# Mixer's output projection taken into the merge's block, and a reordered way from its output to the experts' block table

## The chip, the cores and the metric

The kernel runs on one core of one Trainium2 chip. Its time is the device time of one execution in microseconds (us); a kernel's figure is the median of its runs. The clock of TensorE has two levels, 1.2 and 2.4 GHz; the profile gives the granted clock of a stretch as a share of the upper one.

## What is computed

A block with a token mixer and 64 routed experts, followed by a second block. Only the end of the mixer and the start of the expert stage matter here (512 tokens, width 1024, all float32):

```python
mix, mix_c = token_mixer(...)            # ends in merged @ w_out
x = x + gt1 * rmsnorm(mix, g_post_mix[li])
h = modulate(rmsnorm(x, g_pre_ffn[li]), sh2, sc2)
...
top_g = lax.top_k(grp_score, TOPK_GROUPS)[1]          # 4 of 8 groups
top_e = lax.top_k(jnp.where(emask, sel, -jnp.inf), TOP_K)[1]   # 8 of 64 experts
wts = jnp.take_along_axis(scores, top_e, axis=1)
wts = wts / jnp.sum(wts, axis=-1, keepdims=True) * ROUTED_SCALE
# each expert's tokens are padded to blocks of 128; a table says which token sits in which row
dest = pstart[e_sorted] + jnp.arange(n_assign, dtype=jnp.int32) - start[e_sorted]
buf_tok = jnp.zeros((n_pad,), jnp.int32).at[dest].set(tok_sorted)
...
shared = (jax.nn.silu(h @ w_sh_gate) * (h @ w_sh_up)) @ w_sh_down
```

## The kernel before

The program is written engine by engine, in blocks. Between two blocks all engines meet at a barrier; inside a block they are ordered by semaphores alone. `clear_sems` (L102) clears the semaphores that were used so far, and adds a barrier of its own. Products of full precision are made of three matmuls of rounded parts (`mm3`, L283): every operand is kept as a high part, which ScalarE copies into the rounded type, and a low part, the difference, which VectorE takes. For weights this is the work of `SplitRing`: four raw slots that SyncE fills by DMA, and two pairs of buffers for the parts, so that the parts of tile n need tile n-2 to be used up (`high` L229 to L237, `low` L241 to L248).

The stages around the change, in order of time:

- `merge` (L2790): for each of 8 column tiles (i) four products of 24 matmuls, two for gates and two for the attention and SSD branches; ScalarE takes the sigmoids (L2884), VectorE writes `mergedT[:, i]` (L2953 to L2955). Beside it POOL and VectorE make the late modulation rows in `c.x`, and then POOL loads x again (L2836).
- `project_residual` (L434): merged times w_out, 8 contraction tiles, 4 token tiles and 2 halves of 512 columns, 192 matmuls. The left side is split in two halves (L495, L521) into the buffers of the attention's output. The order is: both column halves for the first four contraction tiles, then for the last four, one half after the other. Only then are the 8 banks copied (L526), squared (L507), the norm's factors made for all tokens at once (L528, L529, POOL L513), and x updated (L533, L538).
- `clear_sems`, then `norm_transpose` (L296): squares of x (L324), factors (L342, POOL L337), scaling (L348), 8 transposes for a token tile (L370), and the way out of the banks with gain and shift by VectorE (L355) and ScalarE (L330) into `hT`. Beside it SyncE runs `ahead` (L3066): the router's weights, constants, the shared expert's weights, and the first expert's weights.
- `experts` (L2981). TensorE: router logits (L3287), 32 matmuls with `hT` as the stationary side and 64 columns; transposes back to token order for the gather (L3294), each tile after ScalarE's copies (L3449) of the one before; then the ranks and counts of the chosen experts (L3305, L3307), the block counts (L3313 to L3315) and the shared expert (L3299, L3332). VectorE: scores, top 4 groups and top 8 experts (L3528 to L3562), the weights `wt` (L3565 to L3569), the keys (L3571, L3573), the counts (L3576 to L3581), the places `dest` (L3584 to L3596), and for each token tile `pick_tile` (L3600 to L3605). POOL: 8 indirect DMAs for a token tile scatter rows into the block table in HBM (L3210), 32 in all, after which the table is loaded (L3212) and the first tokens are gathered (L3192). The expert loop of TensorE begins with the transposes of these rows (L3274).

The second block has the same kind of projection, with a form of the tail that is already written tile by tile: `Rows` (L778), `Turn` (L798), `Residual` (L836), `Tail` (L875), used by `project_norm` (L966). In `Tail` a token tile is squared, normed, added and turned while the next one is multiplied.

```python
    def pe(self, pe, product):
        c, turn = self.c, self.turn
        product(0)
        product(1)
        product(2)
        turn.turn(c, pe, 0)
        product(3)
        turn.turn(c, pe, 1, True)
        turn.turn(c, pe, 2)
        turn.turn(c, pe, 3)
```

## Time and profile before

| | |
|---|---|
| runs | 3293.53, 3294.71, 3296.37 us; median 3294.71 us |
| profiled execution | 3292.3 us |
| span from first to last instruction of that execution | 3290.6 us |
| mean granted TensorE clock | 0.951 |
| PE busy | 3006.1 us (91%) |
| VectorE, ScalarE, POOL busy | 1809.3, 1418.8, 536.1 us |
| chain that ended last | TensorE 11%, all the rest rounds to 0% |

In the profile PE is TensorE's matmuls, PEld its weight loads, DVE is VectorE, ACT ScalarE, POOL GpSimd, SP SyncE; PEq or POOLq is an engine's sequencer. A line such as L3210 is a line of the kernel. One fp32 matmul leaves two matmul records, one of rounded parts leaves one. Times of rows are from the span's start.

### The profile page before, as it was taken

How to read it: one execution, taken by the hardware profiler on the slowest of the kernel's cores; microseconds unless marked ns; L12 is line 12 of the kernel's file. 1: busy time of each engine (PE TensorE's matmuls, PEld its weight loads, DVE VectorE, ACT ScalarE, POOL GpSimd, SP SyncE). 2: the span in 40 equal slices, each digit the busy share in tenths (PEclk: the TensorE clock that was granted, in tenths of full speed). 3: DMA queues.
4: the chain of work that ended last, by engine and by line, in shares of the span. 5: the costliest groups of instructions: out<-in, count | busy, mean ns of one | idle time of the engine just before them, and what ended most of it. 6: DMA issues, size and time to landing. Idle time of an engine off the chain costs nothing. (4 is left out here: it accounts for less than half of the span.)

```text
span 3290.6 us, 37471 instructions
## 1 busy us (share of the span) xinstructions
PE 3006.1 (91%) x14702; PEld 2413.3 (73%) x14702; DVE 1809.3 (55%) x2174; ACT 1418.8 (43%) x1894; POOL 536.1 (16%) x692
## 2 busy tenths in 40 slices
PE   7978899998987799999999689889999899889998
PEld 4866788787876377777777367668887788678887
DVE  4447736445543488888886444555543325445443
ACT  3324526245122288888786122333332334433332
POOL 0005414133100422323222100000000003100000
PEclk9989999998997799999999899889999899999999
DMA  5210201023642279999997630223332211223321
GB/s 193 58 53 1 74 11 52 26 52 122 202 138 90 107 297 367 361 368 373 374 375 299 270 105 1 66 77 103 102 103 77 80 39 52 58 78 90 103 90 51
DMA packets 277406, 455.60 MB, mean 138 GB/s; under 512 B 24656, under 2 KB 206800, under 8 KB 258160
## 3 DMA queue, kind: packets, MB, share of 16 engines
q1 hardware_dynamic: 250832, 398.43, 34.8%
q0 software_dynamic: 26400, 54.79, 4.6%
q8 instruction: 117, 1.92, 0.2%
q14 instruction: 57, 0.47, 0.0%
HBM read 450.77 MB, written 39.08 MB: 149 GB/s over the span
## 5 line engine op out<-in xcount | busy, mean ns | idle before, releaser
L248 DVE TENSOR_TENSOR weight_part<-weights,weight_part 128x2048 fp32r<-128x2048 f32 (+1 forms) x65 | 148.2, 2280 | 166.0 <-ACT weight_part L237 166.0
L288 PE MATMUL banks<-hT_r,weight_part 128*128 128x512 f32 x496 | 200.2, 404 | 4.6 <-PEq L974 2.9
L1133 ACT ACTIVATE up_room<-banks,tap_columns 128x512 f32<-128x512 f32 x88 | 68.6, 779 | 313.9 <-PE banks L293 313.9
L237 ACT ACTIVATE weight_part<-weights 128x2048 fp32r<-128x2048 f32 (+1 forms) x65 | 121.7, 1872 | 174.9 <-PE banks L288 169.4
L1174 DVE SCALAR_TENSOR_TENSOR up_room<-banks,tap_columns,up_room 128x511 f32<-128x511 f32 x88 | 66.0, 750 | 238.5 <-ACT up_room L1133 238.5
L293 PE MATMUL banks<-hT_r,weight_part 128*128 128x512 f32 x496 | 195.5, 394 | 0.0
L248 DVE TENSOR_TENSOR weight_part_o<-weights,weight_part_o 128x2048 fp32r<-128x2048 f32 (+2 forms) x49 | 106.9, 2182 | 143.1 <-ACT weight_part_o L237 143.1
L862 POOL TENSOR_SCALAR branch_mean<-branch_mean 128x1 f32<-128x1 f32 x16 | 3.5, 222 | 1096.7 <-ACT up_room L856 747.2
L288 PE MATMUL banks<-hT_r,weight_part_o 128*128 128x512 f32 x432 | 174.5, 404 | 6.7 <-PEq L105 3.8
L293 PE MATMUL banks<-hT_r,weight_part_o 128*128 128x512 f32 x432 | 170.8, 395 | 0.0
L292 PE MATMUL banks<-h_low,weight_part_o 128*128 128x512 f32 x432 | 169.7, 393 | 0.0
L292 PE MATMUL banks<-h_low,weight_part 128*128 128x512 f32 x432 | 169.0, 391 | 0.0
L3192 POOL DMA_INDIRECT gathered<-h_tokens,block_rows x64 | 115.5, 1805 | 225.0 <-PE banks L3274 206.8
L3269 PE MATMUL banks<-weights_r,gatheredT_r 128*128 128x512 f32 x336 | 133.5, 397 | 0.0
L237 ACT ACTIVATE weight_part_o<-weights 128x2048 fp32r<-128x2048 f32 (+2 forms) x49 | 89.4, 1825 | 98.0 <-PE banks L288 93.7
L288 PEld LDWEIGHTS banks<-hT_r,weight_part 128*128 128x128 f32 x496 | 94.2, 190 | 26.7 <-issue 7.2
L2770 DVE TENSOR_REDUCE minus_maxima<-banks 128x2 f32<-128x1536 f32 x32 | 56.3, 1758 | 97.7 <-PE banks L2679 97.7
L293 PEld LDWEIGHTS banks<-hT_r,weight_part 128*128 128x128 f32 x496 | 93.6, 189 | 22.2
L3517 DVE TENSOR_TENSOR weights_r<-weights,h_tokens_r 128x2048 fp32r<-128x2048 f32 x42 | 95.7, 2291 | 17.5 <-ACT h_tokens_r L3423 17.5
L3268 PE MATMUL banks<-gate_up_high,gatheredT_r 128*128 128x512 f32 x256 | 103.8, 406 | 0.0
L3197 POOL DMA_INDIRECT expert_rows<-lent,block_rows x64 | 65.4, 1022 | 235.3 <-ACT lent L3480 231.3
L3268 PE MATMUL banks<-h_tokens_r,gatheredT_r 128*128 128x512 f32 x256 | 103.2, 403 | 0.0
(725 smaller groups left out, 8977.0 us busy)
## 6 DMA issues: line engine op xcount, KB each, us to landing
weights<-in_w_e_gate SPq DMA_DIRECT2D x44, 1024.0 KB, 15.9
weights<-in_w_e_up SPq DMA_DIRECT2D x44, 1024.0 KB, 18.5
hT<-in_w_e_down SPq DMA_DIRECT2D x44, 1024.0 KB, 18.9
weights<-in_w_up SPq DMA_DIRECT2D x88, 512.0 KB, 5.1
gate_up<-in_w_e_gate SPq DMA_DIRECT2D x22, 1024.0 KB, 15.5
gate_up<-in_w_e_up SPq DMA_DIRECT2D x22, 1024.0 KB, 18.3
down<-in_w_e_down SPq DMA_DIRECT2D x22, 1024.0 KB, 18.4
weights<-in_w_down SPq DMA_DIRECT2D x20, 1024.0 KB, 5.0
```

Source lines behind the costliest of these rows:

```text
L237: c.nc.scalar.activation(self.parts[n % 2][0][:, 0:z], self.raw[n % RAW_SLOTS][:, 0:z], ACT.Copy).then_inc(self.high_ready, 1)
L248: c.nc.vector.tensor_tensor(low[:, 0:z], self.raw[n % RAW_SLOTS][:, 0:z], high[:, 0:z].bitcast(F32), ALU.subtract).then_inc(self.low_ready, 1)
L288: ins = c.nc.tensor.matmul(out, lhs[0], rhs[0], start=start, stop=False)
L292: c.nc.tensor.matmul(out, lhs[0], rhs[1], start=False, stop=False)
L293: return c.nc.tensor.matmul(out, lhs[1], rhs[0], start=False, stop=stop)
L1133: nc.scalar.activation(a[:, f % 2, v], c.ps[:, 2 * (f % 4) + v], ACT.Identity, scale=conv[:, 2, ch:ch + 1], bias=bias[:, ch:ch + 1]).then_ ...
L1174: nc.vector.scalar_tensor_tensor(a[:, f % 2, v, 1:], c.ps[:, 2 * (f % 4) + v, 0:SEQ - 1], conv[:, 1, ch:ch + 1], a[:, f % 2, v, 1:], ALU.m ...
L3192: nc.gpsimd.indirect_dma_start(xg[n % 2][:], None, h_dram, bass.IndirectOffsetOnAxis(tab[:, n, 0:1], 0), bounds_check=SEQ - 1, oob_is_err= ...
L3197: nc.gpsimd.indirect_dma_start(y_dram, bass.IndirectOffsetOnAxis(tab[:, n, 2:3], 0), y[n % 2][:], None, bounds_check=SEQ * TOP_K - 1, oob_ ...
L3268: nc.tensor.matmul(out, lhs[0], rhs[0], start=start, stop=False)
L3269: nc.tensor.matmul(out, lhs[0], rhs[1], start=False, stop=False)
L3517: nc.vector.tensor_tensor(gu_low[i][:, v], gu[i][:, v], gu_high[n % 2][:, v].bitcast(F32), ALU.subtract).then_inc(gu_parted, 1)
```

## The change

Four things are changed; the rest of the program is the same.

1. The projection, the residual and the norm move into the merge's block. `project_residual` and `norm_transpose` go. The weights of w_out follow the merge's own in `SplitRing`; the left side is split in three pieces, contraction tiles 0 to 3, 4 to 6, and 7. The first group is multiplied for both column halves, then the last four contraction tiles are multiplied token tile by token tile in a `Tail` whose outputs are plain (`TurnPlain`, `PlainTail`).
2. `clear_sems` stands ahead of the merge, and no longer behind the projection. The router's and the shared expert's weights are loaded by SyncE at the end of the merge's block (`EarlyExperts`); `ahead` with the rest runs at the start of the experts' block.
3. The router's product has the router's 64 columns as its stationary side and 512 tokens as columns: 8 matmuls, a copy, and four small transposes to token order. The transposes of `hT` use three pairs of banks.
4. On the way to the table, counts come before ranks, ranks are 4 matmuls, the `wt` steps stand behind `dest`, the steps for `over` behind the first `pick_tile`, and the shared expert's matmuls behind the block counts.

```diff
+class TurnPlain(Turn):
+    def weigh(self, c, dve, t):
+        if t >= 2:
+            dve.wait_ge(self.turned, 2 * (t - 1))
+        dve.wait_ge(self.rooted, t + 1)
+        c.nc.vector.tensor_scalar(self.xg[:, t % 2], c.x[:, t], self.rs[:, t:t + 1], None, ALU.mult).then_inc(self.weighted, 1)
...
+class PlainTail(Tail):
...
+    def dve(self, dve):
+        c, res, turn = self.c, self.res, self.turn
+        res.add(c, dve, 0)
+        res.add(c, dve, 1)
+        turn.weigh(c, dve, 0)
+        res.add(c, dve, 2)
+        turn.weigh(c, dve, 1)
+        turn.out_v(c, dve, 0)
+        res.add(c, dve, 3)
+        turn.weigh(c, dve, 2)
+        turn.out_v(c, dve, 1)
+        turn.weigh(c, dve, 3)
+        turn.out_v(c, dve, 2)
+        turn.out_v(c, dve, 3)
...
+        c.clear_sems()
+        merge(c, w_in, h, yT, o_parts, cond, early)
...
                 c.split.load(sp, merge_tiles(c))
-                c.split.ahead(sp, residual_tiles(t["w_out"][0], KD))
+                c.split.load(sp, group_tiles(t["w_out"][0], groups))
+                sp.wait_ge(c.split.low_ready, len(c.split.sizes))
+                early.load(c, sp)
...
+                for hf in range(2):
+                    high, low = group_weights(c, pe, 4)
+                    if hf == 0:
+                        pe.wait_ge(m_low, 1)
+                        pe.wait_ge(left, KD - 1)
+                    for tile in range(NT):
+                        if hf == 0 and tile == 2:
+                            pe.wait_ge(left, KD)
+                        tok = slice(tile * P, (tile + 1) * P)
+                        for j in range(4):
+                            mm3(c, c.ps[:, 2 * tile + hf], [a[:, j, tok] for a in o_parts], (high[:, j], low[:, j]), j == 0, False)
+                pe.wait_ge(m_low, len(pieces))
+                tail.pe(pe, final_product(c, pe, res, [a[:, 4:8] for a in o_parts], 4))
...
+                c.split.high(c, act)
+                act.wait_ge(attn_done, 1)
+                act.wait_ge(left, KD - 1)
+                for n, at in enumerate(pieces):
+                    if n == 2:
+                        act.wait_ge(left, KD)
+                    nc.scalar.activation(o_parts[0][:, at], mT[:, at], ACT.Copy).then_inc(m_high, 1)
+                for _ in range(3):
+                    c.split.high(c, act)
+                tail.act(act)
...
-            pe.wait_ge(landed, 144)
+            pe.wait_ge(early.router_in, 16)
+            for k in range(KD):
+                last = mm1(c.ps[0:E, 0], early.router[:, k], c.hT[:, k], start=k == 0, stop=k == KD - 1)
+            last.then_inc(logits, 1)
+            pe.wait_ge(kept, 1)
             for tile in range(NT):
+                last = nc.tensor.transpose(c.ps[:, 1, tile * E:(tile + 1) * E], by_expert[:, tile * P:(tile + 1) * P], c.ident[0:E, 0:E])
+            last.then_inc(logits_turned, 1)
...
             pe.wait_ge(chosen, 1)
+            pe.wait_ge(landed, 128)
...
-            pe.wait_ge(sh_up_in, 32)
-            shared_up(0, 0, range(0, 2))
             pe.wait_ge(blocked, 1)
...
+            pe.wait_ge(early.up_in, 32)
+            pe.wait_ge(copied, 2 * NT)
+            shared_up(0, 0, range(0, 2))
             shared_up(0, 0, range(2, KD))
```

VectorE at the end of the merge, before (`oT_r` and `oT_low_r` are the parts of the left side, `weight_part` and `hc` the two pairs of weight parts):

```order
L2955 TENSOR_TENSOR mergedT<-mergedT,gated_ssd 128x512
L2798 UNCONDITIONAL_BRANCH
L515 UNCONDITIONAL_BRANCH
L521 TENSOR_TENSOR oT_low_r_3366<-mergedT,oT_r_3365 128x2048
L248 TENSOR_TENSOR weight_part_231<-weights,weight_part_230 128x2048
L248 TENSOR_TENSOR hc_low_r_51<-weights,hc_high 128x2048
```

and now:

```order
L253 TENSOR_TENSOR hc_low_r_51<-weights,hc_high 128x2048
L2828 TENSOR_TENSOR oT_low_r_3366<-mergedT,oT_r_3365 128x2048
L2894 TENSOR_TENSOR gated_ssd<-banks,sigmoids 128x512
L2895 TENSOR_TENSOR mergedT<-banks,sigmoids 128x512
L2896 TENSOR_TENSOR mergedT<-mergedT,gated_ssd 128x512
L2828 TENSOR_TENSOR oT_low_r_3366<-mergedT,oT_r_3365 128x1536
L2828 TENSOR_TENSOR oT_low_r_3366<-mergedT,oT_r_3365 128x512
```

The first weight tile's low part and the first half of the left side stand ahead of the last merge step, and the block's end (the two branches) is gone from between.

TensorE at the start of the experts' block, before (`lent` is a buffer that holds the routing's small arrays):

```order
L3287 MATMUL banks<-weights,hT 128x64 x32
L3294 MATMUL banks<-ident,hT 128x128 x32
L3305 MATMUL banks<-lent 128x64 x10
L3307 MATMUL banks<-lent 64x1 x4
L3299 MATMUL banks<-hT,weights 128x512 x2
L3313 MATMUL banks<-lent 128x64
```

and now:

```order
L3226 MATMUL banks<-hT,weights 64x512 x8
L3230 MATMUL banks<-ident,lent 128x64 x4
L3237 MATMUL banks<-ident,hT 128x128 x32
L3248 MATMUL banks<-lent 64x1 x4
L3250 MATMUL banks<-lent 128x256
L3252 MATMUL banks<-lent 128x192
L3252 MATMUL banks<-lent 128x128
L3252 MATMUL banks<-lent 128x64
L3255 MATMUL banks<-lent 128x64
```

The 32 narrow router matmuls became 8 wide ones, the counts stand ahead of the ranks, and no matmul of the shared expert stands ahead of the block counts.

## Rows read from the trace of the kernel before

**Rows 1.** TensorE in order of time: start, duration, what, [idle before, releaser].

```profile
977.77 0.79 PE L288 MATMUL banks<-weight_part,oT_r 128*128 128x512 f32 x1 [8.84 <-DVE weight_part L248]
...
1045.69 6.43 PE L370 MATMUL banks<-ident,x_scaled 128*128 128x128 f32 x32 [21.06 <-DVE x_scaled L348]
1054.49 13.88 PE L3287 MATMUL banks<-weights,hT 128*128 128x64 f32 x64 [2.37 <-PEq L300]
```

**Rows 2.** ScalarE and VectorE from the scores to the first `pick_tile`.

```profile
1068.41 0.39 ACT L3445 ACTIVATE lent<-banks 128x256 f32<-128x256 f32 x1 [14.23 <-PE banks L3287]
...
1078.02 0.29 DVE L3562 TENSOR_SCALAR lent<-lent 128x256 f32<-128x256 f32 x1
...
1080.14 0.84 DVE L3571 TENSOR_TENSOR_SCAN lent<-lent 128x64 f32<-128x64 f32 x4
...
1087.18 0.15 DVE L3576 COPY lent<-banks 64x1 f32<-64x1 f32 x1 [5.74 <-PE banks L3307]
...
1092.23 0.15 DVE L3592 COPY lent<-banks 64x1 f32<-64x1 f32 x1 [1.23 <-PE banks L3315]
...
1093.76 0.69 DVE L3600 TENSOR_TENSOR lent<-lent 128x512 f32<-128x512 f32 x1
```

**Rows 3.** POOL's scatters into the table, and TensorE's first step of the expert loop.

```profile
1098.22 1.37 POOL L3210 DMA_INDIRECT block_table<-lent  x1 [41.93 <-DVE lent L3605]
...
1121.65 2.93 POOL L3210 DMA_INDIRECT block_table<-lent  x1 [0.31 <-issue]
...
1151.37 1.94 PE L3274 MATMUL banks<-ident,gathered 128*128 128x128 f32 x8 [15.70 <-DMA gathered<-h_tokens,block_rows]
```

**Rows 4.** The page's group of ScalarE's copies of a weight tile: busy, mean ns.

```profile
L237 ACT ACTIVATE weight_part<-weights 128x2048 fp32r<-128x2048 f32 (+1 forms) x65 | 121.7, 1872 | 174.9 <-PE banks L288 169.4
```

**Rows 5.** Stretch: its length, busy (x records) of each engine, PEclk, DMA share, GB/s.

```profile
978.00:983.00 5.00, 5.00 (x13) 3.89 (x14) 2.40 (x2) 3.71 (x2) 0.00 (x0) 0.52 0.00 0
983.00:1025.00 42.00, 41.63 (x181) 33.55 (x179) 11.76 (x11) 8.91 (x16) 0.00 (x0) 1.00 0.00 0
...
1054.40:1068.80 14.40, 14.31 (x67) 14.34 (x68) 0.00 (x0) 0.39 (x1) 1.84 (x2) 0.50 0.67 271
```

**Rows 6.** The second block's `project_norm`, last group and tail, in order of time.

```profile
2138.03 0.40 PE L288 MATMUL banks<-weight_part_o,oT_high 128*128 128x512 f32 x1
...
2142.82 0.50 PE L288 MATMUL banks<-weight_part,oT_high 128*128 128x512 f32 x1 [1.83 <-DVE weight_part L248]
...
2165.28 0.40 PE L293 MATMUL banks<-weight_part,oT_low 128*128 128x512 f32 x1
...
2172.68 1.27 DVE L811 SCALAR_TENSOR_TENSOR tail_rows<-x_tok,rstd,norm_rows 128x1024 f32<-128x1024 f32 x1
...
2174.01 1.97 PE L816 MATMUL banks<-ident,tail_rows 128*128 128x128 f32 x8 [0.42 <-DVE tail_rows L811]
2178.87 0.77 PE L288 MATMUL banks<-hT_r,weight_part_o 128*128 128x512 f32 x1 [2.89 <-PEq L974]
```

**Rows 7.** VectorE and ScalarE in order of time, from the residual to `hT`.

```profile
1032.59 4.63 DVE L538 TENSOR_TENSOR x_tok<-x_tok,yT 128x1024 f32<-128x1024 f32 x4
...
1038.87 1.06 ACT L324 ACTIVATE squares<-x_tok 128x1024 f32<-128x1024 f32 x1 [12.75 <-PEq L105]
...
1050.07 0.74 DVE L348 TENSOR_SCALAR x_scaled<-x_tok,rstd 128x1024 f32<-128x1024 f32 x1
...
1051.28 2.91 ACT L330 ACTIVATE hT<-banks,shift,scale 128x128 f32<-128x128 f32 x8 [0.36 <-PE banks L370]
```

**Rows 8.** The shared expert's fp32 matmuls of 512 columns, two records each.

```profile
1087.00 3.78 PE L3299 MATMUL banks<-hT,weights 128*128 128x512 f32 x4
...
1099.33 20.87 PE L3299 MATMUL banks<-hT,weights 128*128 128x512 f32 x48
```

**Rows 9.** DMA issues from 940 to 1160 us: size, median us to landing.

```profile
lent<-const_table SPq DMA_DIRECT2D x1, 208.0 KB, 6.0
block_table<-lent SPq DMA_DIRECT2D x1, 208.0 KB, 14.8
```

343 lines of the change are left out of this document (120 added, 223 removed).

## The prediction

> **What bounds the kernel now.** I read the page first. TensorE is busy for 91% of the span, so only stretches in which it stands still or is slow can give much. In the slices its granted clock and its busy share fall together at about 1000 to 1150 us, which is the projection's end and the way to the experts. I then read that stretch engine by engine. TensorE's timeline shows the path [rows 1]: it stops at 968.93 with the merge (977.77 less the idle 8.84), starts the projection at 977.77, ends it at 1024.63 (the 1045.69 row less its idle 21.06), waits 21.06 us for the norm, transposes, and starts the router's product at 1054.49. All of this is one chain: each wait is for the last instruction ahead of it. The next group carries it on through VectorE [rows 2]: scores ready at 1068.80, experts chosen at 1078.31, a wait of 5.74 us for TensorE's counts, one of 1.23 us for the block counts, first `pick_tile` at 1093.76. POOL starts its 32 scatters at 1098.22 [rows 3], and the expert loop begins at 1151.37, when the first gathered rows are there. TensorE waited 15.70 us for them, so in that last stretch POOL sets the time and the shared expert lies beside it, with 15.70 us to spare. What is won before 1098.22 moves the whole rest forward; what is won on TensorE behind it is worth nothing.
>
> **The projection and the norm.** Call the start of the router's product T; it is 1054.49 now.
> - From merge to projection. The block's end stands between them now. In the new order the first weight tile's parts and the first half of the left side are made while TensorE still multiplies for the last merge step: attention's product, whose buffers the parts overwrite, ends 5.6 us before the merge's end (24 matmuls at 0.23 us), and ScalarE's copy (1.9 us for such a piece [rows 4]) and VectorE's difference, little longer, fit in that. Token tiles 0 and 1 need banks that are free already, 2 and 3 need the last merge step, which is over 2 us later, while tiles 0 and 1 take 5.5 us. So the 8.84 us go to nothing [rows 1]. With them goes the half clock at the start of the projection: 0.52 in the first 5 us, 1.00 later [rows 5]. At full clock a matmul takes 0.23 us (181 records in 41.63 us); 192 would take 44.4, and took 46.86 (977.77 to 1024.63), so 2.5 us.
> - The first group is 96 matmuls at 0.23 us, 22.2 us, so the last group starts at 968.93 + 22.2 = 991.1.
> - The last group and the tail. The second block runs the same class with the same sizes: from its last group's start, 2138.03, to the next stage, 2178.87, are 40.84 us [rows 6]. In them are a wait of 1.83 us for the second half's weight parts, which the new code has too (the pair of buffers comes free only when the last group begins), and the slow clock behind it. Three things are shorter here. The last tile's scaling takes 0.74 [rows 7] and not 1.27 us [rows 6]; the same on tile 0 brings the first transposes forward, 0.3 us (estimate from that 0.53). Behind the last transposes the second block needs 2.89 us [rows 6]; here ScalarE's four outputs take 1.46 us (half of the eight of 2.91) and the barrier 0.30 (1051.28 + 2.91 to 1054.49) [rows 1, 7], so 1.1 less. That leaves 40.84 - 0.53 - 0.3 - 1.1 = 38.9 us.
> - T = 991.1 + 38.9 = 1030.0, a gain of **24.5 us**. About 11 us of it are the start, the rest is the norm that no longer stands behind the whole product.
>
> **The moved clear.** Where blocks change with a clear, VectorE ends at 1037.22 and ScalarE starts at 1038.87, 1.65 us [rows 7]; without one the barrier is 0.30. The old place is in the 24.5 already. The new one stands ahead of the merge, where TensorE has nothing else: **1.35 us lost**.
>
> **The router.** Now 13.88 us at a granted clock of 0.50, though TensorE is busy all the time [rows 1, 5]. The new form is 8 matmuls of 512 columns. Their price is the shared expert's [rows 8]: 1.89 us at half clock (4 records, two matmuls, in 3.78), 0.87 at full (48 records in 20.87). Before them come transposes at half clock, so I take two at 1.89 and six at 0.87, 9.0 us; the bounds are 7.0 (all full) and 15.1 (all half). Then a copy of 512 columns (0.6, from 0.39 for 256 [rows 2]), four transposes (1.0, half of eight at 1.97 [rows 6]), the sigmoid and the hand-overs (0.6): scores at T + 11.2. Now they are at T + 14.31. Gain **3.1 us**, between 5.1 and -3.0. The Trainium skill (TensorE: Matmul & The Clock Gate, What's actually happening) says that the clock is throttled by default and that activity releases it; the 13.88 us of unbroken matmuls at 0.50 disagree. By that rule the new form takes the 9.0 us and the gain is 3.1; if it goes as the old form did, it is 3.0 lost, and that is the first rival.
>
> **From scores to the first scatter.** The top-k steps are the same: 9.5 us. TensorE's transposes for the gather no longer wait for each copy, and are through about when the experts are chosen. Then the counts are four matmuls of one column, about 1 us (estimate), less than VectorE's scans and keys (1080.14 to 1081.44, where the wait begins: 1.3 us [rows 2]), so the wait of 5.74 goes. Two steps of 0.18 us with their hand-overs (0.15 the bare step [rows 2]) fall away, two of 0.2 go behind the first `pick_tile`. The ranks are 640 columns at 3.7 ns (3.78 us for 1024 [rows 8]), 2.4 us behind the counts; VectorE gets there 1.3 us earlier and waits, in place of the 1.23 for the block counts, which are now made meanwhile. The `wt` steps (1078.31 to 1080.14, 1.8 us [rows 2]) only change places. Gain 5.74 + 0.36 + 0.4 + 1.23 - 1.3 = **6.4 us**.
>
> **At nothing.** The shared expert starts later, behind the block counts: 32 matmuls (two slow) and 16 more, some 50.5 us from the choice, and POOL's rows come at 66.7 (13.5 to the first scatter, which is 1098.22 - 1078.31 less the 6.4, then 53.15 as now), so 16 us of cover stay. Without it each of them would cost its 0.87. The constants are issued at T, 8 DMAs in 4 us, and the last lands 6.0 us behind its issue [rows 9]: T + 10, one us ahead of the scores. The table's first fill (14.8 us [rows 9]) is there by T + 25, the first scatter comes at T + 34. The router's and shared weights are loaded from 996 on, some 30 us before use. The number and length of scatters stay.
>
> **Sum.** 24.5 + 3.1 + 6.4 - 1.35 = 32.6 us, against the profiled execution's 3292.3 us: 3259.7. That execution lies 2.4 us under the median of 3294.71, so for the median I say **3262.1 us**, 1.0% less.
>
> **Rivals.**
> 1. The router stays at half clock. For it: the form now does. Against: the 512-column matmuls of [rows 8] came to 0.87 after a few us. Then 15.1 and not 9.0: 3268.2. Chance 0.10.
> 2. A wait takes the place of the removed ones: the constants. Their DMAs share the rings with 3 MB of weights issued behind them, as the table's first fill does, which took 14.8 us. If the last constant takes that long, it lands at T + 19 and VectorE's first step waits 7.6 us: 3269.7. Against: this constant landed in 6.0 us beside as much traffic [rows 9]. Chance 0.05.
> 3. POOL's small factor steps in the tail wait for VectorE's wide ones. On the last tile's path are two of them; each could wait for at most one instruction of 1.27 [rows 6]: 2.5 us, 3264.6. Against: from the last product's end (2165.68) to the last scaling (2172.68) the second block needs 7.0 us [rows 6], of which nothing looks like a wait. Chance 0.05. The Trainium skill (SBUF — State Buffer, SBUF: two separate sides) states such a rule: VectorE and GpSimd share one pair of ports, and who comes second is blocked for the whole instruction; the 7.0 us agree with it only if no pair meets there.
> 4. Slower: TensorE's clock. If it is granted half from the merge's end on, the 180 matmuls that I count at full clock cost 0.20 us more each, 36 us, the router 6.1 more, and of the shared expert's 45 us more 16 are covered: 3262.1 + 36 + 6.1 + 29 = 3333. It decides from 39.2 us on, that is with projection and router both slow. For it: this stretch has the lowest clock of the program now. Against: there the clock fell in waits, and the projection now follows the merge, at full clock, without one. Chance 0.02.
> 5. The change doesn't do what it says: the tail's order puts a wait on TensorE that leaves the norm behind the product, or the projection is held by the last merge step. Then of the 24.5 only the 11 of the start stay: 3275.6. Against: the second block's rows. Chance 0.03.
>
> **How the numbers follow.** The forecast has 0.75. Its own bounds are the router (2.0 less to 6.1 more), the clock behind the 1.83 us wait (up to 1.6 less if it stays up), the ranks (1 either way), and the scatters, of which one took 2.93 us beside weights being loaded [rows 3], against 1.37 and less: 2 us either way. Range 3254 to 3272, which takes in rivals 1 to 3. A measurement of this kernel tells a change from none at about 0.2%, 6.6 us. Faster by more: 0.96; within: 0.01; slower: 0.03.
>
> **What would show it.** TensorE goes on within 0.3 us of the merge's last matmul and its clock stays at 1.00 until the last group; one wait of about 1.8 us there; 39 us from the last group's first matmul to the router's; the router in 9 us with a clock that rises in it; a wait for TensorE's ranks of about 1.3 us on VectorE and none over 2 us; 32 scatters and 54 us from the first fill to the expert loop, unchanged; 1.7 us between the stages ahead of the merge. I am wrong if TensorE waits again between merge and projection, if more than 7 us lie from the last product to the last scaling, or if the distance from POOL's first scatter to the expert loop grows.

## The result, and the profile of the changed kernel

The changed kernel takes 3259.73 us (median of 4 runs, 3258.22 to 3264.65) against 3294.55 us for the kernel before in the same comparison: ratio 0.9897, 95% interval [0.9882, 0.9911]. It is faster by 1.0%. The forecast was 3262.1 us, with 3254 to 3272 as its range. The profiled execution took 3258.77 us, with a span of 3257.1 us (before: 3292.3 and 3290.6) and a mean granted clock of 0.958 (0.951).

The path around the merge's end first, TensorE in order of time with the two rows of ScalarE and VectorE that stand between (start, duration, what, [idle before, releaser]), in the changed kernel:

```profile
786.08 0.76 PE L293 MATMUL banks<-hT_r,hc_high 128*128 128x512 f32 x1 [2.82 <-PEq L110]
...
996.71 0.50 PE L293 MATMUL banks<-weight_part,oT_r 128*128 128x512 f32 x1 [1.82 <-DVE weight_part L253]
...
1018.98 1.03 ACT L669 ACTIVATE y_high<-banks 128x1024 f32<-128x1024 f32 x1 [2.94 <-PE banks L298]
...
1025.89 0.75 DVE L760 TENSOR_SCALAR y_high<-x_tok,rstd 128x1024 f32<-128x1024 f32 x1 [0.31 <-POOL rstd L608]
...
1030.17 7.05 PE L3226 MATMUL banks<-hT,weights 128*64 128x512 f32 x16 [1.84 <-PEq L2693]
```

The 8.84 us between merge and projection and the 21.06 us behind it [rows 1] are gone: from the first matmul of the merge to the last of the projection TensorE waits once for over 1 us, 1.82 us for the second half's weight parts; behind that product the tail's waits for scaled tiles come to some 5 us. Stretch by stretch (length, busy time and records of PE, PEld, DVE, ACT and POOL, PEclk, DMA share, GB/s):

```profile
970.00:991.00 21.00, 21.00 (x92) 17.08 (x91) 8.81 (x7) 4.36 (x3) 0.00 (x0) 1.00 0.00 1
998.00:1019.50 21.50, 21.50 (x97) 17.40 (x96) 10.13 (x12) 7.34 (x15) 3.96 (x10) 0.94 0.47 157
1019.50:1030.10 10.60, 3.88 (x19) 3.01 (x17) 7.78 (x16) 7.20 (x18) 2.38 (x6) 0.84 0.00 0
1030.10:1037.30 7.20, 7.05 (x16) 2.11 (x16) 0.00 (x0) 0.04 (x1) 1.84 (x2) 1.00 0.19 52
```

The start of the projection runs at 1.00, where it was at 0.52 [rows 5], and so does the router's product, which was at 0.50. Then the way to the first scatter and to the expert loop, in order of time:

```profile
1038.40 0.38 ACT L3391 ACTIVATE lent<-banks 128x256 f32<-128x256 f32 x1 [0.55 <-PE banks L3230]
...
1040.19 0.42 DVE L3474 TENSOR_TENSOR lent<-lent 128x256 f32<-128x256 f32 x1 [10.97 <-DMA lent<-const_table]
...
1053.23 0.42 DVE L3525 TENSOR_SCALAR lent<-banks 128x256 f32<-128x256 f32 x1 [1.32 <-PE banks L3252]
...
1063.28 1.12 POOL L3150 DMA_INDIRECT block_table<-lent  x1 [31.31 <-DVE lent L3551]
...
1116.15 1.94 PE L3214 MATMUL banks<-ident,gathered 128*128 128x128 f32 x8 [15.99 <-DMA gathered<-h_tokens,block_rows]
```

The waits of 5.74 and 1.23 us [rows 2] are gone, one of 1.32 us for the ranks has come. A wait that the forecast did not have stands ahead of VectorE's first step: the scores are there at 1038.78, the last constant a good us later, and the step starts at 1040.19. TensorE's wait for the gathered rows is 15.99 us, as the 15.70 of [rows 3].

The expert loop begins 35.2 us earlier than before, the span is 33.5 us shorter. Of the missing 1.7 us, 1.4 lie in the expert loop. The record of its first to last transposes of gathered rows is shown for the changed kernel and for one of the experiments below, in which only another clear of semaphores is added (x count: duration ns min/median/max, first and last start, forms):

```profile
L3214 PE MATMUL banks<-ident,gathered x544: 270/272/448, 1116.1 to 1786.7; 128*128 128x128 f32 x182
```

```profile
L3217 PE MATMUL banks<-ident,gathered x544: 270/273/446, 1117.2 to 1785.0; 128*128 128x128 f32 x182
```

That is 670.6 and 667.8 us; the kernel before has 669.2, and over all profiles here the same loop takes from 667.1 to 673.8 us. Nothing of it is the change. It is also why medians of four runs say little about the small steps below, which are therefore read from each kernel's profile, stage by stage.

### The profile page after: what moved, and what is told of

Read it like the earlier page. It is cut to its first block and busy times, and to the rows that moved or that the text cites. A ratio compares the mean times of both kernels' runs of the same rounds, so it can differ in the third digit from the quotient of the medians.

```text
span 3257.1 us, 37329 instructions
## 1 busy us (share of the span) xinstructions
PE 2989.0 (92%) x14646; PEld 2393.1 (73%) x14646; DVE 1804.4 (55%) x2162; ACT 1417.4 (44%) x1888; POOL 546.0 (17%) x706
## 6 DMA issues: line engine op xcount, KB each, us to landing
weights<-in_w_e_gate SPq DMA_DIRECT2D x44, 1024.0 KB, 10.7
```

## The experiments

Twelve kernels ran beside the two. This table holds what their profiles say, worked out from rows like those above, in us; there is one profile for each kernel. T is the start of the router's product. "Merge" is the merge's first matmul, so that what lies ahead of it does not count. Up to T nothing differs between the changed kernel (both times), undo_router, undo_routing, undo_both, shared_more and routing_better, and their distances from merge to T (244.1 to 245.1) show how far one such figure repeats.

| kernel | merge to T | last product to T | router | T to first step of the choice | first step to first scatter | first scatter to expert loop | merge to expert loop | median, ratio to before with interval |
|---|---|---|---|---|---|---|---|---|
| before | 269.7 | 29.9 | 13.9 | 14.4 | 29.3 | 53.2 | 366.6 | 1 |
| changed | 244.1 | 11.2 | 7.05 | 10.0 | 23.1 | 52.9 | 330.1 | 3259.73, 0.9897 [0.9882, 0.9911] |
| changed_again | 245.1 | 11.6 | 7.05 | 10.4 | 23.1 | 52.3 | 330.9 | 3260.17, 0.989 [0.9869, 0.9912] |
| late_start | 254.5 | 11.6 | 9.0 | 10.7 | 23.1 | 52.2 | 340.5 | 3267.98, 0.9913 [0.9897, 0.993] |
| norm_behind | 255.6 | 23.7 | 8.6 | 10.7 | 23.1 | 53.0 | 342.4 | 3271.25, 0.9926 [0.991, 0.9943] |
| undo_router | 244.2 | 11.6 | 13.9 | 14.4 | 22.7 | 52.4 | 333.8 | 3262.64, 0.9896 [0.988, 0.9913] |
| undo_routing | 245.1 | 11.6 | 7.05 | 10.8 | 25.3 | 51.7 | 332.9 | 3263.04, 0.9903 [0.9886, 0.9919] |
| undo_both | 244.2 | 11.6 | 13.9 | 14.4 | 29.3 | 53.2 | 341.1 | 3268.35, 0.9922 [0.9905, 0.9938] |
| shared_more | 244.2 | 11.6 | 9.0 | 10.7 | 23.1 | 64.8 | 342.8 | 3272.24, 0.9933 [0.9917, 0.995] |
| double_clear | 243.9 | 11.2 | 7.05 | 9.9 | 23.1 | 52.3 | 329.2 | 3263.22, 0.9906 [0.9887, 0.9924] |
| routing_better | 244.2 | 11.6 | 9.0 | 10.7 | 21.8 | 53.5 | 330.1 | 3259.74, 0.989 [0.9873, 0.9906] |
| tail_order | 241.4 | 11.6 | 8.9 | 10.6 | 23.1 | 52.2 | 327.2 | 3256.04, 0.9884 [0.9867, 0.99] |
| best | 241.0 | 11.5 | 8.7 | 10.4 | 21.7 | 54.5 | 327.6 | 3260.1, 0.9887 [0.9864, 0.991] |
| held_loads | 241.1 | 11.6 | 8.8 | 10.5 | 21.8 | 60.2 | 333.5 | 3263.32, 0.9907 [0.989, 0.9924] |

**late_start.** The projection's first parts only after the last merge step.

```diff
-                        pe.wait_ge(left, KD - 1)
+                        pe.wait_ge(left, KD)
...
-                c.split.high(c, act)
                 act.wait_ge(attn_done, 1)
-                act.wait_ge(left, KD - 1)
+                act.wait_ge(left, KD)
+                c.split.high(c, act)
...
-                        c.split.low(c, dve)
-                        m_part(0)
                     dve.wait_ge(done, i + 1)
...
+                c.split.low(c, dve)
+                m_part(0)
                 m_part(1)
```

> The changed kernel with one part undone: the first parts of w_out and of the left side are made only after the last merge step, and TensorE waits for that step ahead of token tile 0. Theory (the terms of the forecast add up): TensorE waits again between merge and projection, for VectorE's last merge step (2.0 us), ScalarE's high part (1.9 us) and VectorE's two low parts (2.3 us each), 8.5 us, and the clock may fall in that wait and cost up to 2.5 us more: 8.5 to 11 us slower than the changed kernel, all of it at the start of the router's product. Rival (the clock is the larger part of the gain): once TensorE has waited, its clock stays low through the last group and the tail as well, and the loss is over 14 us. Rival (the start was hidden): the last group's own waits take it up and the loss is under 4 us.

Measured: T comes 10.4 us later (254.5 against 244.1). Its first projection matmul, in order of time:

```profile
981.39 0.77 PE L293 MATMUL banks<-hc_high,oT_r 128*128 128x512 f32 x1 [8.68 <-DVE oT_low_r L2828]
```

A wait of 8.68 us, where 8.5 were worked out. Behind it the clock needs the first 5 us to come back (0.69 there, 1.00 in the rest of the first group), and the first group takes 23.6 us and not 22.1: 1.4 us. The last 0.3 us lie behind the last product. (The merge took 1.5 us more than in the changed kernel and the last group 1.6 us less; that is the clock too and not this edit, as the last section shows.) So the start is worth some 10 us, and the clock is its smaller part; it did not stay low.

**norm_behind.** The norm waits for the whole product.

```diff
 class PlainTail(Tail):
+    def pe(self, pe, product):
+        c, turn = self.c, self.turn
+        for t in range(NT):
+            product(t)
+        for t in range(NT):
+            turn.turn(c, pe, t, t == 1)
...
     def act(self, act):
+        act.wait_ge(res.done, NT)
```

> The changed kernel with one part undone: all four token tiles are multiplied first, ScalarE's first square waits for the last of them, and all transposes stand behind. Theory (the rest of the 24.5 us, beyond the start's 11, is the norm that no longer stands behind the whole product): VectorE has some 19 us of work for the four tiles (two wide steps of the residual, a scaling and four outputs each), with 2 to 3 us ahead of it, and now only 11.2 us lie behind the last product: 9 to 13.5 us slower than the changed kernel. Rival (the tail is bound by something else, such as POOL's roots or the outputs of the last tile): under 4 us slower.

Measured: 11.5 us later at T; from the last product to T 23.7 us instead of 11.2. TensorE now waits 8.79, 2.09, 2.77 and 0.37 us for the four scaled tiles, and from its first step of the residual to its last output VectorE is busy for 17.9 of 20.2 us, so its work for the tiles is the bound, as expected. The rival, a tail bound elsewhere, is out.

**undo_router.** The router's product in its old form.

```diff
-            for k in range(KD):
-                last = mm1(c.ps[0:E, 0], early.router[:, k], c.hT[:, k], start=k == 0, stop=k == KD - 1)
-            last.then_inc(logits, 1)
-            pe.wait_ge(kept, 1)
-            for tile in range(NT):
-                last = nc.tensor.transpose(c.ps[:, 1, tile * E:(tile + 1) * E], by_expert[:, tile * P:(tile + 1) * P], c.ident[0:E, 0:E])
-            last.then_inc(logits_turned, 1)
+            for tile in range(NT):
+                for k in range(KD):
+                    last = mm1(c.ps[:, 1, tile * E:(tile + 1) * E], c.hT[:, k, tile * P:(tile + 1) * P], early.router[:, k], start=k == 0, stop=k == KD - 1)
+            last.then_inc(logits, 1)
```

> The changed kernel with one part undone: the router's product in its old form, 32 products of 64 columns with the tokens as the stationary side, and no copy and turning of the scores. Theory (the form sets the clock: the old one runs at half clock however it is started): 13.9 us of matmuls, scores at T + 14.3 instead of a first VectorE step at T + 10.0, 4.3 us slower than the changed kernel. Rival (the old form was slow only because TensorE had waited 21 us ahead of it; here it starts at full clock): 7 us of matmuls, scores at T + 7.5, VectorE held by the constants until T + 10 as now, so no difference (0 to 1 us).

Measured: 13.89 us of matmuls and the first step at T + 14.4: 4.4 us later than in the changed kernel, both as in the kernel before. The windows of this kernel, the tail's end and the router:

```profile
1029.00:1033.60 4.60, 2.41 (x11) 1.62 (x10) 3.33 (x9) 3.02 (x8) 0.03 (x1) 0.50 0.00 0
1033.60:1047.40 13.80, 13.79 (x65) 13.80 (x66) 0.00 (x0) 0.00 (x0) 1.82 (x2) 0.50 0.51 197
```

and those of late_start, in which the new form was met by a half clock too:

```profile
1042.00:1047.00 5.00, 5.00 (x8) 1.47 (x9) 0.00 (x0) 0.00 (x0) 1.77 (x2) 0.61 0.25 68
1047.00:1051.00 4.00, 3.96 (x10) 1.04 (x8) 0.00 (x0) 0.00 (x0) 0.00 (x0) 1.00 0.40 142
```

Busy without a gap in both, the old form stays at 0.50 to its end and the new one is back at 1.00 inside 5 us. The rival wanted the old form to start at full clock; here the clock had fallen ahead of it. The nearest look at that is the kernel before, in its wait of 2.37 us ahead of the router and in the router:

```profile
1053.00:1054.40 1.40, 0.00 (x0) 0.00 (x0) 0.36 (x2) 1.18 (x4) 0.00 (x0) 1.00 1.08 396
1054.50:1068.30 13.80, 13.80 (x65) 13.80 (x66) 0.00 (x0) 0.00 (x0) 1.79 (x2) 0.50 0.69 281
```

The clock was at 1.00 until the old form began and at 0.50 from its first matmuls on. Whether the form or the wait ahead of it did that is not shown.

**undo_routing.** The steps behind the choice in their old order (TensorE's part is shown; VectorE's goes back as the change's diff has it, the pick's buffers apart).

```diff
-    TURNED_AT = (6, 4, 2, 6)
+    TURNED_AT = (6, 6, 6, 6)
...
-                if tile == 3:
-                    pe.wait_ge(copied, 2)
+                if tile:
+                    pe.wait_ge(copied, 2 * tile)
...
+            for tile in range(NT):
+                for j in range(tile + 1):
+                    mm1(c.ps[:, 1, tile * E:(tile + 1) * E], tri[:, LT if j == tile else ONES], mask[:, j], start=j == 0, stop=j == tile)
             for j in range(NT):
-                last = mm1(c.ps[0:E, 0, 7 * E:7 * E + 1], mask[:, j], tri[:, ONES, 0:1], start=j == 0, stop=j == NT - 1)
+                last = mm1(c.ps[0:E, 1, NT * E:NT * E + 1], mask[:, j], tri[:, ONES, 0:1], start=j == 0, stop=j == NT - 1)
             last.then_inc(counted, 1)
...
+            shared_up(0, 0, range(0, 2))
             pe.wait_ge(blocked, 1)
```

> The changed kernel with the steps from the choice to the first scatter in their old order: the gather's transposes in one pair of banks, each waiting for the copies of the one before; ranks in ten products ahead of the counts; two of the shared expert's products ahead of the block counts; wt steps ahead of the keys; the first block numbers ahead of the first pick. Theory (forecast's terms): 6.4 us slower than the changed kernel, first wait of VectorE behind the keys near 5.7 us less the 1.8 of the wt steps put back ahead of it. Rival (the transposes are no part of it, because they now begin 9 us ahead of the choice and end with it even when they wait for the copies): the wait for the counts is only what ranks and counts take on TensorE, 5.4 us less 3.1 of VectorE's own steps, and the loss is 4 to 5 us.

Measured: only 2.3 us (25.3 against 23.1), less than either side had. VectorE's waits on the way:

```profile
1042.51 0.42 DVE L3473 TENSOR_TENSOR lent<-lent 128x256 f32<-128x256 f32 x1 [12.06 <-DMA lent<-const_table]
1057.55 0.15 DVE L3521 COPY lent<-banks 64x1 f32<-64x1 f32 x1 [2.51 <-PE banks L3251]
1061.85 0.15 DVE L3537 COPY lent<-banks 64x1 f32<-64x1 f32 x1 [0.48 <-PE banks L3259]
```

The old order waits 2.51 and 0.48 us here and not 5.74 and 1.23. Two things favour it: VectorE starts the choice 2.1 us behind the scores because of the constants, while TensorE's transposes do not wait for them, and those run partly at full clock (the first tile's pass takes 3.1 us, where each takes 3.9 to 4.0 in the kernel before). The two come to 3.4 us, of the 4.0 that are missing.

**undo_both.** Router and routing together; the diff is the two above.

> The changed kernel with the router in its old form and the steps from the choice to the first scatter in their old order, both at once. Apart they cost: first VectorE step of the choice from T + 10.0 to T + 14.4 (the router), and from there to the first scatter 23.1 to 25.3 us (the order), where the kernel before needs 29.4. Theory (the two are not independent: the constants' wait of VectorE and the clock that the new router leaves behind gave the old order a lead of some 4 us that it does not have by itself): together 29.4 us from the first step to the first scatter, a wait of VectorE for the counts near 5.7 and one near 1.2 us, T + 14.4 for the first step, so 10.7 us slower than the changed kernel. Rival (the terms are independent, and the missing 4 us came from something else that both kernels share): 25.3 us to the first scatter, a wait near 2.5 us, 6.6 us slower.

Measured:

```profile
1046.54 0.43 DVE L3468 TENSOR_TENSOR lent<-lent 128x256 f32<-128x256 f32 x1 [15.70 <-ACT lent L3385]
1064.83 0.15 DVE L3516 COPY lent<-banks 64x1 f32<-64x1 f32 x1 [5.77 <-PE banks L3248]
1069.88 0.15 DVE L3532 COPY lent<-banks 64x1 f32<-64x1 f32 x1 [1.24 <-PE banks L3256]
```

The old waits are back, 5.77 and 1.24 us, and 29.3 us to the first scatter as before. From T to the first scatter undo_router needs 37.2 us, undo_routing 36.1 and this kernel 43.8, where the changed kernel needs 33.1. Undone apart the two parts cost 4.0 + 3.0 = 7.0 us (0.8 of the 3.0 because the constants landed later in that execution); together 10.6. The theory holds: what one part is worth depends on the other.

**shared_more.** The shared expert's third product five times over.

```diff
-            shared_up(1, 0, range(KD))
+            for _ in range(5):
+                shared_up(1, 0, range(KD))
```

> The changed kernel with 32 more matmuls of 512 columns in the shared expert (one of its four products is done five times over; its result stays the same): at 0.87 us each 27.8 us more on TensorE behind the choice. Theory (the shared expert lies beside POOL's scatters with 16 us to spare): TensorE's wait of 16.0 us for the first gathered rows goes, 11.8 us come on top, 3271.5 us. Rival (the gathered rows are late because TensorE's weight loads and ScalarE's copies slow the scatters, and more matmuls slow them further): over 14 us more. Rival (the wait is not cover but the path goes elsewhere, as through the weights of the first experts): under 8 us more, or all 27.8.

Measured: from the first scatter to the loop 64.8 us, 11.9 more; the time is 3272.24. TensorE's wait for the rows is gone, it waits 1.11 us for ScalarE's last eviction instead. The cover of 16 us is real, and behind it each matmul costs its 0.87.

**routing_better.** The constants of VectorE's first steps on their own semaphore and first, and the wt steps in the wait for the ranks.

```diff
+        sp.dma_start(bias, t["router_bias"].to_broadcast([P, E])).then_inc(first_in, 16)
+        sp.dma_start(small, t["rank"].to_broadcast([P, 72])).then_inc(first_in, 16)
         for i, m in enumerate((0, 3, 4)):
...
-            dve.wait_ge(landed, 128)
+            dve.wait_ge(first_in, 32)
...
+            L(V.tensor_tensor(wt, sg, mask, ALU.mult))
...
+            L(V.tensor_tensor(wt, wt, tot.unsqueeze(2).to_broadcast([P, NT, E]), ALU.mult))
             dve.wait_ge(ranked, 1)
```

> The changed kernel with the two waits filled that its own trace shows on the way to the first scatter: the router's bias and the rank table are loaded first and on their own semaphore, so that VectorE's first step waits for the scores alone (wait of 1.4 us, T + 8.6 instead of T + 10.0), and the wt steps (1.8 us) stand in the wait for the ranks (1.3 us). Theory: both lie on the path, the first scatter comes 2.7 us earlier from T (T + 30.4 instead of T + 33.1), and the time falls by as much, to about 3257.0 us. Rival (the next wait is right behind: with the choice earlier, the other constants or TensorE's transposes, which end at T + 12.4, hold the counts or the keys): less than 1 us is left at the first scatter. Rival (POOL waits for the block table's first fill): no gain at all.

Measured: the wait for the ranks is gone, 21.8 us instead of 23.1 to the first scatter. The other half shows nothing here: in this execution the router took 9.0 us, the scores came at T + 10.6, and VectorE was held by them. The 1.3 us did not reach the expert loop, because first scatter to loop took 53.5 instead of 52.9 us and T + 10.6 stood for T + 10.0. The time is that of the changed kernel.

**tail_order.** Another order inside the last group.

```diff
+    def pe(self, pe, product):
+        product(0, (0,))
+        product(1, (0,))
+        product(0, (1,))
+        product(1, (1,))
+        product(2)
+        product(3)
+        turn.turn(c, pe, 0)
+        turn.turn(c, pe, 1, True)
+        turn.turn(c, pe, 2)
+        turn.turn(c, pe, 3)
...
-        turn.out_a(c, act, 0)
         res.square(c, act, 3, rows)
         square(2)
-        turn.out_a(c, act, 1)
+        turn.out_a(c, act, 0)
         square(3)
+        turn.out_a(c, act, 1)
```

> The changed kernel with the order inside the projection's last group changed: token tiles 0 and 1 with the first half of the columns, then both with the second half, so that the second half's weight parts (4.2 us on ScalarE and VectorE) are ready when TensorE comes to them, and all four transposes behind the last product; ScalarE squares tile 3 ahead of its outputs. Theory (from the last product on, T follows by a chain of 11.2 us whose steps each wait only for the one before, and the second-half wait of 1.8 us and the first tile's transposes, 1.1 us with a wait of 0.3, stand ahead of that product): last product's end and T come 3 to 4 us earlier, last group's start to T 34 to 35 us instead of 38.1. Rival (VectorE and ScalarE are the bound there: two wide steps, a scaling and four outputs each for four tiles, which all wait for the transposes now): the chain behind the last product grows to 14 us or more and nothing is gained. Rival (the clock): the 1.8 us are taken back by a lower clock in the last group.

Measured: no wait for weight parts, the last product ends 3.1 us and T comes 2.7 us earlier, a little less than the 3 to 4 expected; the chain from the last product to T is 11.6 us, as in nearly all of these kernels. The last group's start to T is 34.0 us. Of the 4.3 us less than in the changed kernel only 3.0 are the new order, since the kernels with the old order whose clock stayed at 1.00 there need 37.0. Both rivals are out: the clock is at 1.00 through the whole last group. Expert loop 2.8 us earlier, median 3256.04 us, the lowest of all; but the interval of its ratio, [0.9867, 0.99], overlaps that of the changed kernel.

**best.** Both together.

> The changed kernel with both improvements of the earlier runs at once: the new order of the last group and of the transposes, which brought the router's start 2.8 us forward, and on the routing path the constants of VectorE's first steps loaded first, and the wt steps in the wait for the ranks, which took 1.3 us off. Theory (one chain, the two add up): last product's end to T 11.55 us as before, T 241.3 us after the merge's first matmul, first step to first scatter 21.7 us, expert loop 326 us after the merge's first matmul against 330.1: 4.1 us less than the changed kernel. Rival (not additive: an earlier choice meets TensorE's transposes or the table's first fill): 2.8 us or less.

Measured: T at 241.0 and 21.7 us to the first scatter, both as expected, so the parts add up that far. Then 54.5 us to the loop instead of 52.9 take 1.6 back: the loop starts at 327.6 and not at 326, a gain of 2.5 us. That lies in the rival's range, but neither cause that the rival named is it. POOL in this kernel, its last scatter and the read of the finished table:

```profile
1102.70 0.96 POOL L3164 DMA_INDIRECT block_table<-lent  x1 [0.30 <-issue]
1108.51 0.60 POOL L3166 DMA_DIRECT2D block_rows<-block_table  x1 [4.86 <-DMA block_table<-lent]
```

The scatters are done earlier but land later: 4.86 us, where the changed kernel has 2.99. Median 3260.1 us: no gain that can be told.

**changed_again.** The changed kernel once more.

> The changed kernel itself, unchanged, to be measured beside the improved one and to see how far its profile repeats. Theory (the router started at half clock in five of the executions profiled so far, 8.6 to 9.0 us, and the 7.05 us of the first profile are the rarer case): router 9.0 us, scores at T + 10.6, no wait for the constants beyond that, expert loop some 0.6 us later from the merge than in the first profile. Rival (the 7.05 us are the changed kernel's own, and the experiments' edits moved the clock): router 7.05 us and a wait of 1.4 us for the constants again.

Measured: the rival's figures. The router took 7.05 us again, and VectorE waited until T + 10.4 for the constants. The expert loop comes 0.8 us later from the merge: 1.0 more up to T, 0.3 more for the constants, 0.5 less behind the first scatter. That the 7.05 us are the changed kernel's own is not shown by that: shared_more, whose one edit stands behind the router, took 8.98, and undo_routing and double_clear took 7.05.

**double_clear.** A second clear behind the moved one.

```diff
         c.clear_sems()
+        for i in range(8):
+            c.sem(f"spare{i}")
+        c.clear_sems()
         merge(c, w_in, h, yT, o_parts, cond, early)
```

> The changed kernel with a second clear of semaphores (eight spare ones) behind the one ahead of the merge, and nothing else. Theory (a clear with its barrier costs what the trace of before showed, 1.65 us against 0.30 for a bare one, and the moved one costs the difference): TensorE's wait ahead of the merge grows from 2.82 by 1.2 to 1.7 us, and the time by as much, which the runs can't tell apart. Rival (the price is in the number of semaphores that are cleared, and eight cost little): under 0.5 us.

Measured: TensorE's wait ahead of the merge is 3.26 us instead of 2.82, which is what all the other changed kernels have, so 0.44 us more. That is the rival: a clear has no fixed price of 1.35 us. How it grows with the number of semaphores one point does not tell.

**held_loads.** The best kernel, with the next experts' weights held until the scatters have landed.

```diff
-            sp.wait_ge(sh_up, 2)
-            gate_up(2)
-            down(1)
-            down(2)
             sp.wait_ge(sh_down, NT)
+            sp.wait_ge(sent, 16 * NT * TOP_K)
             gate_up(1)
+            down(1)
+            gate_up(2)
+            down(2)
```

> The improved kernel (both improvements) with one more edit: the weights of experts 1 and 2, which SyncE now loads as soon as the shared expert's products are through (3 MB and then 2 MB beside POOL's scatters), are held until all 32 scatters of the block table have landed. In the changed kernel two scatters beside that load stand 2.6 and 2.2 us apart instead of 1.27, and the table's read starts 3.0 us after the last scatter's end; in the improved kernel that last gap is 4.9 us. Theory (the load slows the scatters and the landing of the last ones): all scatters 1.3 us apart, the last gap under 2.5 us, first scatter to expert loop 48 to 50 us instead of 54.5 and 52.9, so 3 us or more less than the changed kernel has there. Rival (the load then meets the table's read and the first gathers, or the weights come late for experts 1 and 2): the scatters are faster, but the first gathered rows land later or TensorE waits for weights in the first experts, and nothing is left at the third expert.

Measured: half of each. POOL again, first its slow scatters, then the last one and what follows:

```profile
1085.26 2.33 POOL L3164 DMA_INDIRECT block_table<-lent  x1 [0.30 <-issue]
1087.89 1.90 POOL L3164 DMA_INDIRECT block_table<-lent  x1 [0.30 <-issue]
...
1101.45 0.95 POOL L3164 DMA_INDIRECT block_table<-lent  x1 [0.30 <-issue]
1103.83 0.60 POOL L3166 DMA_DIRECT2D block_rows<-block_table  x1 [1.43 <-DMA block_table<-lent]
1110.99 1.05 POOL L3146 DMA_INDIRECT gathered<-h_tokens,block_rows  x1 [6.55 <-DMA block_rows<-block_table]
```

Without a load beside it the last scatter lands after 1.43 us (in shared_more, where the loads came later too, 1.42). But the table's read then meets the held loads, 6.55 us instead of 2.73, and the gathers as well: 60.2 us to the loop, 5.7 more than in best. And the two slow scatters are there with no load beside them (DMA share 0.01 from 1084.4 to 1089.8), so the load was not their cause.

## Why the prediction was right, and where it was not

The time was right to 2.4 us, the mechanism of each large term held, and three statements behind the terms were wrong.

- **The start and the tail, 24.5 us.** Measured from the merge's first matmul, T came 25.6 us earlier. The parts undone cost 10.4 us (forecast about 11) and 11.5 us (the rest, 13.5); 3.7 us belong to neither alone: the undone kernels keep the rest of the new code, and 0.5 lie in the merge itself, which took 183.7 us and not 184.2. Last group's start to T is 38.3 us (991.91 to 1030.17), forecast 38.9; the slow clock behind the 1.82 us wait, which the forecast took over from the second block, was there and cost 1.6 us, the size that it had given as a bound. (192 matmuls at 0.23 us are 44.2 us and not 44.4; nothing in the sum rests on it.)
- **The clear, 1.35 us.** TensorE's wait ahead of the merge is 2.82 against 1.63: 1.2 us. The size was right for this place; double_clear shows that it is no general price.
- **The router, 3.1 us.** Mis-sized, on the good side: the first step came at T + 10.0 and not T + 11.2, so 4.4. The 9.0 us were right in kind and found so in seven experiments (8.6 to 9.0). In the changed kernel, both times, the clock was back at 1.00 ahead of the router, and it took 7.05. The copy, four transposes and sigmoid took 1.6 and not 2.2. Rival 1, a router that stays at half clock, was not seen; the old form in the new place did just that. The rule of the Trainium skill (TensorE: Matmul & The Clock Gate, What's actually happening), that activity releases the clock, holds for the new form and not for the old, in which TensorE is as busy.
- **The constants, "one us ahead of the scores".** Wrong. They landed at T + 10.0, as said, but the scores were there at T + 8.6, since the router was quicker; VectorE waited 1.4 us. It is rival 2 in a small form (it had 7.6 us): a wait took the place of a removed one. Of the 2.6 us that scores come earlier than forecast, 1.4 were lost there.
- **Scores to first scatter, 6.4 us.** Measured 29.3 - 23.1 = 6.2. The sum was right, its attribution was not. The wait of 5.74 us "goes", by the forecast, because the transposes no longer wait for copies. That holds only against the old router's clock: with the new router the old order waited 2.51 us and cost 2.3 us behind VectorE's first step. The new wait for the ranks, 1.32 us, was forecast at 1.3.
- **At nothing.** The cover of 16 us is 15.99 in the row, and shared_more shows it used up at the price named. First scatter to expert loop 52.9 against 53.15. That the 2.93 us scatter was slow "beside weights being loaded" is refuted by held_loads.
- **Rivals 3 and 5** are out. From the last product's end to the last scaling are 6.95 us (1018.94 to 1025.89), under the 7 us that were set as the limit, and POOL's steps there take 0.22 and 0.57 us each, none longer. TensorE does not wait at the projection. Rival 4 is out as well: the clock in this stretch rose.

## What to carry over

Undo the parts of a change one at a time and all together: here two parts were worth 7.0 us apart and 10.6 together, because the clock and a late DMA had moved the engines against each other. Ahead of a queue of fixed length (here POOL's 32 scatters) what is won counts as far as that length holds (51.7 to 54.5 us from the first scatter to the loop where no edit touched it), and what lies beside it counts only from where its cover ends. When a stage is made quicker, look at what the next one waits for beside it: here the constants took back 1.4 of the 2.6 us. That loading them first and on their own semaphore pays was not shown, since in routing_better and best the scores held VectorE.

## What the hardware did that was not expected

**VectorE's wide steps stretch POOL's indirect DMAs.** Most of the scatters are issued 1.26 us apart and take 0.96 us each; two are far longer. Around them in the changed kernel, VectorE's rows first, then POOL's:

```profile
1085.96 2.28 DVE L3463 TENSOR_TENSOR gate_up_r<-gate_up,gate_up_high 128x2048 fp32r<-128x2048 f32 x1
...
1088.16 2.28 DVE L3463 TENSOR_TENSOR gate_up_r<-gate_up,gate_up_high 128x2048 fp32r<-128x2048 f32 x1
```

```profile
1085.50 0.96 POOL L3150 DMA_INDIRECT block_table<-lent  x1 [0.30 <-issue]
1086.76 2.32 POOL L3150 DMA_INDIRECT block_table<-lent  x1 [0.30 <-issue]
1089.38 1.90 POOL L3150 DMA_INDIRECT block_table<-lent  x1 [0.30 <-issue]
1091.58 0.96 POOL L3150 DMA_INDIRECT block_table<-lent  x1 [0.30 <-issue]
```

And in the kernel before:

```profile
1121.46 2.29 DVE L3517 TENSOR_TENSOR gate_up_r<-gate_up,gate_up_high 128x2048 fp32r<-128x2048 f32 x1
...
1123.67 2.29 DVE L3517 TENSOR_TENSOR gate_up_r<-gate_up,gate_up_high 128x2048 fp32r<-128x2048 f32 x1
```

```profile
1121.65 2.93 POOL L3210 DMA_INDIRECT block_table<-lent  x1 [0.31 <-issue]
1124.89 1.90 POOL L3210 DMA_INDIRECT block_table<-lent  x1 [0.30 <-issue]
```

The slow pair begins inside the two steps of 2.28 us in which VectorE takes expert 0's weights apart, both inputs from SBUF, and it stands at the same place in the kernel before and in all the others but one. In before, undo_both, tail_order, best and held_loads VectorE starts at 1121.46, 1099.33, 1085.38, 1085.71 and 1084.47, the first slow scatter 0.2 to 0.8 us behind it, at whatever number it then is (the 18th to the 21st). The ends fit too: VectorE's steps end at 1088.24 and 1090.44 and the slow scatters at 1089.08 and 1091.28, each 0.84 us behind a step's end (0.83 in the kernel before, both times), as if most of a scatter's 0.96 us had to wait for that end. In shared_more VectorE comes to these steps only at 1114.84, when the scatters are through, and there none is slow. Against two scatters 1.26 us apart the pair costs POOL 2.3 us on the path, 2.9 where the first takes 2.9. The Trainium skill (SBUF — State Buffer, SBUF: two separate sides) says that VectorE with two inputs from SBUF and a GpSimd instruction that reads SBUF take turns on a shared pair of ports, each for a whole instruction. The ends above agree with it; that the scatters are held at that pair, and not by something else that VectorE's steps bring, no run here shows. It was cited ahead of the result for the tail, where it did not show, and overlooked here. In shared_more the last scatter ends 40.9 us after the first one's start, in the changed kernel 43.2. Moving the steps behind the last scatter by itself is the next thing to try; it wasn't tried.

**The clock's fall lands differently.** In kernels whose code is the same from the merge to the router the clock fell and rose in different places (us; the merge goes from its first matmul to the projection's, the router is the new form):

| kernel | merge | first group | last group | last product to T | router |
|---|---|---|---|---|---|
| changed | 183.7 | 22.1 | 27.0 | 11.2 | 7.05 |
| changed_again, undo_routing | 184.4 | 22.1 | 27.0 | 11.6 | 7.05 |
| double_clear | 185.2 | 22.1 | 25.4 | 11.2 | 7.05 |
| shared_more, routing_better | 185.0 | 22.1 | 25.4 | 11.6 | 9.0 |

The first three have a slow clock behind the wait for the second half's weight parts, the others have not. The same 5 us of the last group in the changed kernel and in routing_better:

```profile
996.00:1001.00 5.00, 4.29 (x12) 3.42 (x13) 0.65 (x1) 0.00 (x0) 0.00 (x0) 0.66 0.62 163
```

```profile
997.30:1002.30 5.00, 4.25 (x19) 3.49 (x19) 0.69 (x1) 1.12 (x2) 0.01 (x1) 1.00 0.64 163
```

That costs 1.6 us. The merge is shorter in these three because the clock is back sooner at its start: 0.53 in the first 3 us and 1.00 in the next 3 in the changed kernel, 0.50 and 0.55 in shared_more. In all of them, and in late_start and norm_behind, the clock falls to 0.50 behind the long wait of the tail. It was back at 1.00 when the router began in changed, changed_again, undo_routing and double_clear, and at 0.50 in the other kernels of this study with a new or an old router. What decides it is open, and with one profile for each kernel it can't be told whether it belongs to the kernel or to the execution. It moved single stages by up to 2 us, but merge to T by 1 us at most, and the scores' 2 us reached the path with 0.7 because of the constants. So a stage that is compared between two profiles is compared with its clock beside it.
